# A ring of ten expert tiles, attention turns last in their slot, and a column of ones

## What is computed

```python
def expert_choice_moe(h, w_router, w_gate_e, w_up_e, w_down_e):
    ...
    top_aff, idx = lax.top_k(jnp.swapaxes(affinity, 1, 2), cap)
    ...
    hid = jax.nn.silu(jnp.einsum('becd,edf->becf', xe, w_gate_e)) * jnp.einsum('becd,edf->becf', xe, w_up_e)
    ye = jnp.einsum('becf,efd->becd', hid, w_down_e)
    return jnp.zeros_like(h).at[bidx, idx].add(ye * top_aff[..., None].astype(ye.dtype))

def fox_mixer(h, w_in, b_f, w_out):
    ...
    logf = jax.nn.log_sigmoid((fl + b_f).astype(jnp.float32))
    c = jnp.cumsum(logf, axis=1).transpose(0, 2, 1)
    ...
        logits = logits + (cqi[..., :, None] - c[:, :, None, :])
        ...
        p = jax.nn.softmax(logits, axis=-1)
        return jnp.einsum('bhqk,bhkd->bhqd', p.astype(v.dtype), v)
```

## Time and profile before

| | |
|---|---|
| runs shown, us | 3379.48, 3381.28, 3382.33 (median 3381.28) |
| profiled execution, us | 3377.78, of which the span of the trace 3376.0 |
| TensorE (PE) busy | 3294.2 us, 98% |
| VectorE (DVE) busy | 1675.6 us, 50% |
| ScalarE (ACT) busy | 1166.8 us, 35% |
| mean granted clock of TensorE | 0.992 of 2.4 GHz |
| moved by DMA | 624.02 MB, mean 185 GB/s |

### The profile page before, as it was taken

One profiled execution on the slowest core, in us unless ns is written; L12 is line 12 of the kernel. 1 busy time (PEld: TensorE's weight loads), 2 busy tenths in 40 slices (PEclk: granted clock), 3 DMA queues, 4 the chain that ended last, 5 costly groups with the idle time before them and its releaser, 6 DMA issues.

```text
span 3376.0 us, 41358 instructions
## 1 busy us (share of the span) xinstructions
PE 3294.2 (98%) x17120; PEld 2360.7 (70%) x17120; DVE 1675.6 (50%) x2538; ACT 1166.8 (35%) x1816; POOL 93.9 (3%) x75
## 2 busy tenths in 40 slices
PE   8999999999989999999999999999999999999998
PEld 6778886444447768886444447777888888778887
DVE  4764542212146774552112126446756674676665
ACT  5653322010126653322100125445433354453333
POOL 0000000000001000000000000001000010010000
PEclk9999999999999999999999999999999999999999
DMA  6112259999973112257999992321233222223222
GB/s 194 54 55 79 79 192 362 427 427 427 427 321 122 58 55 71 72 206 294 427 427 427 427 389 69 113 76 51 100 100 100 88 93 70 75 65 109 92 96 75
DMA packets 275449, 624.02 MB, mean 185 GB/s; under 512 B 11120, under 2 KB 208528, under 8 KB 225856
## 3 DMA queue, kind: packets, MB, share of 16 engines
q1 hardware_dynamic: 274736, 621.06, 48.6%
q10 hardware_dynamic: 528, 0.32, 0.0%
HBM read 612.93 MB, written 8.42 MB: 184 GB/s over the span
## 4 chain that ended last, share of the span: by engine, by line
PE 83%; DVE 8%; DMA 4%; ACT 3%; issue 1%; POOL 0%; SPq 0%; POOLq 0%; DVEq 0%; ACTq 0%
PE bank L2456 17%; PE bank L477 17%; PE bank L479 16%; PE bank L478 16%; PE bank L2437 3%; DMA expert_w<-in_w_exp_up 3%; DVE w_lo L207 1%; DVE raw_lo L662 1%; DMA expert_w<-in_w_exp_down 1%; PE bank L1552 1%; DVE h_plain L721 1%; ACT w_hi L199 1%; PE bank L1516 1%; PE bank L2491 1%; PE bank L2857 1%
## 5 line engine op out<-in xcount | busy, mean ns | idle before, releaser
L477 PE MATMUL bank<-h_hi,w_hi 128*128 128x512 f32 x1752 | 696.1, 397 | 9.8 <-DVE w_lo L207 8.0
L479 PE MATMUL bank<-h_hi,w_lo 128*128 128x512 f32 x1752 | 684.3, 391 | 0.0
L478 PE MATMUL bank<-h_lo,w_hi 128*128 128x512 f32 x1752 | 683.7, 390 | 0.0
L207 DVE TENSOR_TENSOR w_lo<-w_raw,w_hi 128x2048 fp32r<-128x2048 f32 (+3 forms) x209 | 423.9, 2028 | 155.9 <-ACT w_hi L199 155.1
L2456 PE MATMUL bank<-expert_w,gathered 128*64 128x512 f32 x2016 | 445.5, 597 | 10.1 <-DMA expert_w<-in_w_exp_up 10.0
L199 ACT ACTIVATE w_hi<-w_raw 128x2048 fp32r<-128x2048 f32 (+3 forms) x209 | 355.5, 1701 | 230.7 <-PE bank L479 198.4
L477 PEld LDWEIGHTS bank<-h_hi,w_hi 128*128 128x128 f32 x1752 | 329.8, 188 | 93.1 <-issue 16.3
L479 PEld LDWEIGHTS bank<-h_hi,w_lo 128*128 128x128 f32 x1752 | 329.7, 188 | 70.5
L478 PEld LDWEIGHTS bank<-h_lo,w_hi 128*128 128x128 f32 x1752 | 330.1, 188 | 67.5 <-issue 1.9
L2456 PEld LDWEIGHTS bank<-expert_w,gathered 128*64 128x64 f32 x2016 | 143.9, 138 | 293.5 <-issue 287.5
L2456 PE MATMUL bank<-expert_w,hidden_t 128*64 128x512 f32 x1024 | 226.7, 595 | 1.2 <-DMA expert_w<-in_w_exp_down 1.2
(11 more groups left out here) (440 smaller groups left out, 4727.6 us busy)
## 6 DMA issues: line engine op xcount, KB each, us to landing
expert_w<-in_w_exp_up SPq DMA_DIRECT2D x64, 2048.0 KB, 22.1
expert_w<-in_w_exp_down SPq DMA_DIRECT2D x64, 2048.0 KB, 23.6
expert_w<-in_w_exp_gate SPq DMA_DIRECT2D x62, 2048.0 KB, 23.3
w_raw<-in_ffn_w_up SPq DMA_DIRECT2D x44, 1024.0 KB, 4.9
w_raw<-in_w_branch_gate SPq DMA_DIRECT2D x64, 512.0 KB, 3.8
w_raw<-in_ffn_w_down SPq DMA_DIRECT2D x22, 1024.0 KB, 4.9
w_raw<-in_w_in SPq DMA_DIRECT2D x20, 1024.0 KB, 5.1
w_raw<-in_hgrn_w_in SPq DMA_DIRECT2D x16, 1024.0 KB, 5.1
```

Source lines behind the costliest of these rows:

```text
L207: dve.tensor_tensor(self.w_lo[n % 2][:, 0:e], self.raw[n % self.RAW][:, 0:e], self.w_hi[n % 2][:, 0:e].bitcast(F32), ALU.subtract).then_in ...
L477: pe.matmul(out, st[0], mv[0], start=(j == 0), stop=False)
L478: pe.matmul(out, st[0], mv[1], start=False, stop=False)
L479: last = pe.matmul(out, st[1], mv[0], start=False, stop=(j == len(g.steps) - 1))
```

## The change

The ring of expert tiles gets a tenth place, at 103 KB from the layer's base. In the ring's order it is the fifth, so the places that followed it move by one. Tile 5 is now issued by `side_loads` after the load of the first of the four output-weight tiles, without a wait, and the order at the start of `moe` is 0, 6, 7, stores, 9, 10, 8. From tile 11 on, tile g waits until g - 9 tiles are used. In an attention slot TensorE does values, scores, turns. The tile `ones_row` and its memset are gone (2 KB a partition, so the layer's base lies lower); the scans read one column of `ones` with a step of 0, and the logarithm takes its bias from there. The scratch of software-issued transfers has the same size before and after.

```diff
-        dve.memset(v.ones_row[:], 1.0)
...
         first = n - (len(tiles) - 3)
+        if first == -1:
+            loads.issue(sp, 5)
         if first == 0:
             sp.wait_ge(*sig("group_summed").ge(gate_groups))
...
-    places = [v.layer_base, v.layer_base + size, v.h_base, v.layer_base + 2 * size, v.layer_base + 3 * size, v.h_base + size] + [
+    places = [v.layer_base, v.layer_base + size, v.h_base, v.layer_base + 2 * size, v.layer_base + 103 * K, v.layer_base + 3 * size, v.h_base + size] + [
         v.ring_base + i * size for i in range(3)]
...
-    NT, RING, EARLY = 12, 9, 4
+    NT, RING, EARLY = 12, 10, 5
...
-            for g in (0, 5, 6):
-                if g == 6:
+            for g in (0, 6, 7):
+                if g == 7:
                     sp.wait_ge(*norm.summed.ge(1))
                 loads.issue(sp, g)
             products.store(sp)
             sp.wait_ge(*products.all_summed)
-            for g in (8, 9):
+            for g in (9, 10):
                 loads.issue(sp, g)
             sp.wait_ge(*products.all_stored)
-            loads.issue(sp, 7)
+            loads.issue(sp, 8)
             for g in range(RING + 1, NP * NT):
                 sp.wait_ge(*at(used, 0, g - RING + 1))
                 loads.issue(sp, g)
...
-            order(dve.tensor_tensor_scan(other, chosen, v.ones_row[0:NE, :], 0.0, ALU.add, ALU.mult))
+            order(dve.tensor_tensor_scan(other, chosen, v.ones[0:NE, 0:1].to_broadcast([NE, S]), 0.0, ALU.add, ALU.mult))
...
         for u in self.at_step(slot, 3):
             self.values(pe, u)
+        for u in self.at_step(slot, 0):
+            self.scores(pe, u)
         for u in self.at_step(slot, 2):
             self.turn(pe, u)
-        for u in self.at_step(slot, 0):
-            self.scores(pe, u)
...
-            dve.tensor_tensor_scan(t[1][:], t[2][:], v.ones_row[0:H, :], 0.0, ALU.add, ALU.mult).then_inc(*rows_ready.inc())
+            dve.tensor_tensor_scan(t[1][:], t[2][:], v.ones[0:H, 0:1].to_broadcast([H, S]), 0.0, ALU.add, ALU.mult).then_inc(*rows_ready.inc())
...
-            act.activation(t[2][:], t[1][:], ACT.Ln, bias=v.ones_row[0:H, 0:1]).then_inc(*f_act.inc())
+            act.activation(t[2][:], t[1][:], ACT.Ln, bias=v.ones[0:H, 0:1]).then_inc(*f_act.inc())
...
-        v.ones_row = sb("ones_row", [P, S])
```

## The result

The changed kernel takes 3363.62 us (median of four runs, 3363.01 to 3365.98), the kernel before beside it 3381.81 (3379.48 to 3382.94): ratio 0.9950, 95% interval 0.9937 to 0.9962. In the profiled executions the span fell from 3376.0 to 3361.2 us, by 14.8.

The account below looks back on a forecast made before the run. TensorE, busy nearly everywhere, was held to lose time to late expert tiles and a lowered clock. Gains of 6.42 and 4.91 us, all else 0, summed to 11.3: 3377.78 to 3366.5 profiled, 3370 from the median; range 3366 to 3377.

Parts of the forecast that it names:

- The tenth tile: Expert stages: each tile lands 4.91 us earlier, saving 6.42 us in layer 0 and 4.91 in layer 1.
- the head start of the prediction: Before the expert stages: a tile sent while transfers idle is worth its length, 4.91 us, at the stage's end.
- What is late next: End of each expert stage: some 1.1 to 1.5 us of wait stays, now for the last down tile.
- The issue itself: Mixer's end: second output-weight tile lands at worst 4.91 us later, 4.7 hidden by slack; cost 0 to 0.2, taken as 0.
- The gain goes on past the stage: Behind layer 0's expert stage: VectorE's gate-weight split is not late, so what follows moves as a whole; sum 11.3 us.
- The row of ones: Routers and forget gates: three scans reading one column cost 0; bounds a 1.6 us gain, a 3.6 us loss.
- Turns last: Attention slots, scores before turns: taken as 0; bounds a gain of 1.8 us, a loss of 2.0.
- Both layers lose the clock: Rival, expert stages: lowered clock in layer 1 too, 1.56 us more given back; gain 12.9, time 3368.4; chance 0.10.
- Head start lost: Rival, expert stages: the early tile only lengthens the pause at 545 to 555 us; gain 0 to 5; chance 0.11.
- Early tile starves the mixer's end: Rival, mixer's end: second output-weight tile late, TensorE stands still; at 8 us a layer 3386 us; chance of slower 0.04.
- slower scans: Rival, routers and forget gates: scans, with later exponentials, at their bounds give 3376 us; chance 0.05 for small edits' bounds.

Follow-up runs that it names:

- x2: The changed kernel with the old order (values, turns, scores) in the attention slots: 3369.80 us, ratio 0.9970 to the kernel before.
- x6: The changed kernel with tile 5 issued only behind tile 0 at the expert stage's start: 3370.36 us, ratio 0.9969 to the kernel before.
- x8: The changed kernel itself, timed a second time in more rounds: 3365.77 us, ratio 0.9957 to the kernel before.
- x3: The kernel before with only the row of ones replaced by the column: 3378.59 us, ratio 0.9999 to the kernel before.
- x1: The kernel before with only the forgetting attention's slot order changed to values, scores, turns: 3375.21 us, ratio 0.9984.
- x7: The changed kernel with scores put before turns in the mixer's two attentions too: 3356.06 us, ratio 0.9926 to the kernel before.
- x5: The changed kernel with the attention slot order scores, values, turns: 3367.04 us, ratio 0.9961 to the kernel before.

## Why the direction was right and the size short

- **The tenth tile: right, mechanism and size.** 6.2 and 5.2 us in the trace for 6.4 and 4.9, and no single trace's luck: the three traces with nine places have stages of 439.5 to 441.3 us in layer 0 and 439.1 to 440.4 in layer 1, the eight with ten and the early issue 433.9 to 435.8 and 434.4 to 435.9. In layer 0 the last landing is at 944.89 + 33.20 = 978.09, 3.1 late like the whole stage, so 975.0 on the old scale, forecast 974.81. By the 358 GB/s of the Trainium skill (DMA: Bandwidth & Descriptors, Where 436 GB/s comes from) the sum would have been 13.2; the ring gave 11.4 in the trace and 10.1 (6.8 to 13.5) in the runs of x2, which can't tell them apart, but the transfers again ran at 423 to 427. How much of it is the head start of the prediction and how much the pause that a tenth place fills, x6 leaves open.
- **What is late next: right in size, partly in place.** A wait for downs ends each stage (0.5; 1.4 in two pieces); layer 0 also keeps 0.8 for an up tile. In x8, the same kernel, there is no wait for an up tile, and the waits for downs are 1.2 and 1.7.
- **The issue itself: right.** 2.8 us late at the output weights, nothing of it seen by TensorE.
- **The gain goes on past the stage: right.** VectorE's split of the first gate-weight tile starts at 983.38, 1.56 behind the stage's end, as before.
- **The row of ones: right.** 1.21 us a scan; x3 puts the whole edit at 0 (0.9990 to 1.0007).
- **Turns last: this step failed**, as "I take 0; bounds: a gain of 1.8". It measured 5.4 us in the trace and 5.4 (2.4 to 8.4) in the runs of x1. I looked for the gain only in TensorE's waits, where 1.8 was the most there could be, and took a busy TensorE as one with nothing to give. The order changed what TensorE does between its products: 0.163 us less in a slot. Of the 5.4, 4.8 are the order's. From the third mask product to the last one it takes 179.75 to 179.77 us in the three traces of the old order (before, x2, x3), and 174.89 to 174.97 in the five of the new one (x1, after, x6, x7, x8). The remaining 0.6 is luck: the first two slots last 13.9 us in after, 14.9 in before, but up to 17.0 in other traces of the new order, whose wait for maxima there is 0.6 to 2.2 us. The Trainium skill (Perfetto Trace Analysis, Identifying the Most-Contended Engine) warns that the busy share of TensorE's products is a poor measure and points, among others, to the busy share of the weight loads. The trace agrees with the warning: TensorE showed 98% before and after. The weight loads' busy share did not show it either, 70% before and after. With 4.8 to 5.4 in place of 0 the sum is 16.1 to 16.7 and the time 3365.2 to 3364.6.
- **Rivals.** *Both layers lose the clock*: true in x3, half true in before, not in x1, so it is a matter of the run; but its 1.56 us for layer 1 did not show, and in the traces it moves the kernel before by 1.5 to 1.8 us in layer 0. The rule of the Trainium skill (TensorE: Matmul & The Clock Gate, Part 1), by which the rival had each such wait cost clock, was borne out in three of six waits. *Head start lost*: not in the kernel after, where the pause kept its size; that it is there to be filled at all, x6 shows. *Early tile starves the mixer's end* and *slower scans*: no trace of either.

The 3.1 us by which the first expert product came later in the profile of after is a matter of that execution: in x8, the same kernel, it came at 544.01, and in x6 at 544.09. Some 1.4 of it are there by 64 us, and some 1.6 come in the mixer's slot at 205 us, in which TensorE stood 1.9 us and then ran at the lower clock.

## What to carry to other kernels

Small products between large ones cost what their neighbours make them cost: put those with the same weights' shape side by side, and count the changes in a slot. A gain from a new order need not come out of any wait, so do not call a stage full because its products fill it. Take the weight loads' idle time as a hint of where to look, and judge by the period of a slot in a stretch without waits: it repeated to 0.001 us here, where whole times spread over some us. A place more in a ring pays by what can be sent ahead of the stage or, with nothing sent ahead, by the pause that it fills: 5.2 and 3.7 us of layer 1's stage in two traces here.

## What the hardware showed unexpectedly

A weight load ran ahead of the products before it where the weights had the same shape, and started with its own product where the shape changed; a change avoided was worth 0.14 to 0.17 us in most places, 0.08 between mask and values in x5, and the two orders differed by 0.016 when the values had the shape of the turns. A change of place without one of shape shows no such cost: the values' products go by turns to the two halves of the output's rows, and their twelve loads of 0.137 us follow one another within 0.64 us. And after long waits for an up tile in the same place the clock fell in three cases and not in three: after 3.4 us but not after 3.7 in before, after both waits of 3.1 in x3 and after neither of 3.1 in x1.
